# The modulation moves into the first FFN stage: sections 0 to 2 at its start, sections 3 to 8 on GpSimd and TensorE beside its products

## The chip, the core and the metric

One core of a Trainium2 chip runs the whole program. The metric is the device time in microseconds. The kernel before takes 3244.37 us, the median of three runs from 3243.7 to 3245.0 us.

## The reference, cut to what matters

One layer on 128 context tokens and 1024 latent tokens, D_MODEL 1024, D_FF 2816, all in float32. The modulation is a vector of nine sections of 1024 numbers for each of the two conditions (context and latents), and every sub-layer uses three of them.

```python
mod = (jax.nn.silu(c) @ ada_w[l] + ada_b[l]).reshape(b, 9, 1024)    # for c_ctx and for c
h = rmsnorm(x, norm_w[0]) * (1.0 + m[1]) + m[0]
x = x + 0.5 * m[2] * swiglu(h, ffn1_w13, ffn1_w2)       # first FFN: sections 0, 1, 2
h = rmsnorm(x, norm_w[1]) * (1.0 + m[4]) + m[3]
x = x + m[5] * token_mixer(h, ...)                      # sections 3, 4, 5
h = rmsnorm(x, norm_w[2]) * (1.0 + m[7]) + m[6]
x = x + 0.5 * m[8] * swiglu(h, ffn2_w13, ffn2_w2)       # sections 6, 7, 8
```

## The kernel before

`program` (L1936 to L1963) runs stage after stage with a barrier between any two (L81): the modulation, ffn1, the mixer's stages, ffn2, the final norm. The activations are held transposed in `x`: eight tiles of 128 features by 1152 tokens, in three chunks of CH = 384 tokens (CH and NC, L20 and L21).

**The modulation** (`modulation`, L94 to L224) handles one section at a time. SP loads a section of `ada_w` with four DMAs of 1 MB into one of two buffers (L121), and x (L126) between sections 1 and 2. TensorE multiplies the silu of both conditions by it, 16 matmuls in four column groups (L176), each two instructions in the trace. ScalarE copies the rows to SBUF (L154), and TensorE turns them with a 0/1 matrix `select`, eight small matmuls (L187), so that a section stands along the partitions. VectorE adds the bias (L210). After the ninth section it makes the scales and gates (L218, L221).

**ffn1 and ffn2** are one function, `hidden_stage` (L348), with the norm as its first part. `Norm` (L227): ScalarE, VectorE and GpSimd square x, TensorE sums the squares over the features with a matrix of ones (L275), ScalarE takes the root (L286), VectorE the reciprocal (L335). Then tile after tile of x, 24 in all: VectorE makes `x_normed` (L340), ScalarE the high half `h_hi` (L297), GpSimd the full value `h_full` (L313), and VectorE the low half `h_lo` by subtraction (L325). Products are made of high and low halves, three matmuls for each. In chunk 0 a tile has two token segments, one per condition.

The body goes over 22 tiles of D_FF in eleven pairs. A pair has six up blocks (par, c), of 48 matmuls each (L558), and three down blocks, of 48 matmuls (L573); the order on TensorE is up (0,0), down of the pair before chunk 2, up (0,1), up (0,2), up (1,0), up (1,1), down chunk 0, up (1,2), down chunk 1 (DOWN, L369). Pair 0 has no first down block. Around them, per up block: ScalarE's silu (L606), VectorE's product g (L609), ScalarE's `g_hi` (L440), VectorE's `g_lo` (L494), and the splits of the next weight tiles into `whi` (L428) and `wlo` (L466), which SPLITS (L366) hands out. VectorE adds a down block to x with the gate (L474). SP loads the weight tiles a, b and d, one ahead (L402). GpSimd does nothing in the body of ffn1. Each engine's program runs in order, and the semaphores alone tie them together.

Of the kernel before, what the change touches and what calls it, by code (L numbers as in the profile page):

```python
# [93 lines left out]
def modulation(kit):  # L94

    nc = kit.nc
    loaded_vec, loaded_x, loaded_select = kit.sem("vec_loaded"), kit.sem("x_loaded"), kit.sem("select_loaded")  # L100
    loaded = [[kit.sem(f"ada_loaded{p}{g}") for g in range(4)] for p in range(2)]
    cleared, silu_ready, ones_ready = kit.sem("cond_cleared"), kit.sem("silu_ready"), kit.sem("ones_ready")
    rows_done, rows_ready, turned = kit.sem("mod_rows_done"), kit.sem("mod_rows_ready"), kit.sem("mod_turned")
    section_added, section_done = kit.sem("section_added"), kit.sem("section_done")
    HALF = D // 2
    with ExitStack() as ctx:
        raw = ctx.enter_context(nc.sbuf_tensor("ada_raw", [P, 2, 4, 2, D], F32))
        cs = ctx.enter_context(nc.sbuf_tensor("cond_silu", [P, KT, 32], F32))
        rows = ctx.enter_context(nc.sbuf_tensor("mod_rows", [P, 2, 2, HALF], F32))
        select = ctx.enter_context(nc.sbuf_tensor("select", [P, 2], F32))  # L110
        block = ctx.enter_context(nc.Block())

        @block.sync
        def _(sp):
            sp.dma_start(kit.vec[:], kit.dram["vec"]).then_inc(loaded_vec, 16)

            def section(i, par, first=False):
                if not first:
                    kit.hold(sp, rows_done, i * 2 - 2)
                for g in range(4):  # L120
                    sp.dma_start(raw[:, par, g], kit.dram["ada_w"][i, g]).then_inc(loaded[par][g], 16)  # L121
            section(0, 0, True)
            sp.dma_start(select[:], kit.dram["select"]).then_inc(loaded_select, 16)
            section(1, 1, True)
            for k in range(KT):
                sp.dma_start(kit.x[:, k, :], kit.dram["xT"][k]).then_inc(loaded_x, 16)  # L126
            section(2, 0)
            with sp.Fori(1, 4) as i:
                for par in range(2):
                    section(i * 2 + (1 + par), 1 - par)  # L130
            sp.wait_ge(loaded_x, 16 * KT)

        @block.gpsimd
        def _(pool):
            pool.memset(cs[:], 0.0).then_inc(cleared, 1)
            pool.memset(kit.ones[:], 1.0).then_inc(ones_ready, 1)
            pool.memset(kit.eps[:, 0:1], NORM_EPS).then_inc(ones_ready, 1)
            pool.memset(kit.eps[:, 1:2], GN_EPS).then_inc(ones_ready, 1)

        @block.scalar  # L140
        def _(act):
            act.wait_ge(loaded_vec, 16)
            act.wait_ge(cleared, 1)
            a = PACK["c"][0]
            for cond in range(2):
                nc.scalar.activation(cs[:, :, cond], kit.vec[:, a + 8 * cond:a + 8 * cond + 8],
                                     ACT.Silu).then_inc(silu_ready, 1)

            def section(i, par, first=False):
                for half in range(2):  # L150
                    act.wait_ge(rows_done, i * 2 + (half + 1))
                    if not first and half == 0:
                        act.wait_ge(turned, i - 1)
# [10 lines left out]
        def _(pe):  # L164
            pe.wait_ge(silu_ready, 2)

            def section(i, rank, par, first=False):
# [3 lines left out]
                if not first:  # L171
                    pe.wait_ge(rows_ready, i * 2 - 2)
# [1878 lines left out]
```

## Time and profile before

| | us |
|---|---|
| median of 3 runs | 3244.37 |
| the profiled execution, its own time | 3243.18 |
| its span | 3241.4 |
| last section of the modulation added | 119.3 |
| first FFN product | 149.3 |
| last FFN product of ffn1 ends | 989.0 |

The page of the profile gives the busy share of each engine and, in 40 slices of 81 us, when it was busy and how busy the DMA engines were. TensorE is busy 92% of the span, VectorE 45%, ScalarE 24%, GpSimd 10%. PEclk is the granted TensorE clock; 1.00 is 2.4 GHz. PE is TensorE, PEld its weight loads, DVE VectorE, ACT ScalarE, POOL GpSimd, SP SyncE. The order of time gives start and duration of each instruction or run of equal ones; the DMA issue of an engine is listed under SPq, and its duration is that of the issue, not of the transfer.

### The profile page before, as it was taken

The numbers are of one execution on the slowest core, as the hardware profiler recorded it, in microseconds if no ns is written. First come the engines' busy times: TensorE is split into PE (matmuls) and PEld (weight loads), VectorE is DVE, ScalarE is ACT, GpSimd is POOL, SyncE is SP. The second block draws the span as 40 slices with busy tenths as digits, with TensorE's granted clock in tenths as the row PEclk, the third lists the DMA queues.
The fourth block names the chain that finished last, engine by engine and source line by source line (L and its number), as shares of the span: only waits on it lengthen the run. The fifth ranks groups of instructions, "written<-read, shape, count | busy, mean of one in ns | idle before, by whom it ended". The sixth has DMA issues, their size and how long they took to land. (4 is left out here: it accounts for less than half of the span.)

```text
span 3241.4 us, 56108 instructions
## 1 busy us (share of the span) xinstructions
PE 2975.2 (92%) x23416; PEld 2787.4 (86%) x23416; DVE 1456.3 (45%) x2475; ACT 776.3 (24%) x1296; POOL 332.4 (10%) x318
## 2 busy tenths in 40 slices
PE   4799999999996999998699976989979999999997
PEld 1399999999995988998588954779879999999996
DVE  0344333334436345432688855335553343443335
ACT  0321111111113233443133334212141111111112
POOL 0310000000004001122121212012240000000000
PEclk7899999999998999999799998989999999999999
DMA  9411111111102334443444321242111111111111
GB/s 399 159 40 39 39 39 39 57 50 42 39 13 90 129 107 149 164 156 138 116 109 96 68 107 33 71 172 93 44 36 46 39 39 39 39 39 39 39 40 64
DMA packets 182217, 263.72 MB, mean 81 GB/s; under 512 B 78128, under 2 KB 133424, under 8 KB 177456
## 3 DMA queue, kind: packets, MB, share of 16 engines
q1 hardware_dynamic: 182064, 261.52, 24.5%
q8 instruction: 116, 1.90, 0.2%
q14 instruction: 37, 0.30, 0.0%
HBM read 206.35 MB, written 55.12 MB: 81 GB/s over the span
## 5 line engine op out<-in xcount | busy, mean ns | idle before, releaser
L474 DVE SCALAR_TENSOR_TENSOR x<-bank,gate,x 128x128 f32<-128x128 f32 (+1 forms) x832 | 411.6, 516 | 209.6 <-PE bank L573 209.1
L609 DVE TENSOR_TENSOR g_ffn<-act_out_ffn,bank 128x384 f32<-128x384 f32 x132 | 73.2, 554 | 742.7 <-ACT act_out_ffn L606 742.7
L558 PE MATMUL bank<-h_hi_ffn,wlo_a_ffn 128*128 128x384 f32 x1056 | 356.9, 338 | 21.2 <-DVE h_lo_ffn L325 11.3
L606 ACT ACTIVATE act_out_ffn<-bank 128x384 f32<-128x384 f32 x132 | 65.0, 492 | 1246.1 <-PE bank L558 1246.0
L558 PE MATMUL bank<-h_lo_ffn,whi_a_ffn 128*128 128x384 f32 x1056 | 355.8, 337 | 0.0
L558 PE MATMUL bank<-h_hi_ffn,whi_a_ffn 128*128 128x384 f32 x1056 | 355.5, 337 | 0.0
L573 PE MATMUL bank<-g_hi_ffn,wlo_d_ffn 128*128 128x384 f32 x1056 | 352.9, 334 | 2.4 <-DVE g_lo_ffn L494 2.4
L573 PE MATMUL bank<-g_hi_ffn,whi_d_ffn 128*128 128x384 f32 x1056 | 352.7, 334 | 0.0
L558 PE MATMUL bank<-h_hi_ffn,whi_b_ffn 128*128 128x384 f32 x1056 | 352.7, 334 | 0.0
L573 PE MATMUL bank<-g_lo_ffn,whi_d_ffn 128*128 128x384 f32 x1056 | 352.7, 334 | 0.0
L558 PE MATMUL bank<-h_hi_ffn,wlo_b_ffn 128*128 128x384 f32 x1056 | 352.7, 334 | 0.0
L558 PE MATMUL bank<-h_lo_ffn,whi_b_ffn 128*128 128x384 f32 x1056 | 352.7, 334 | 0.0
L1066 PE MATMUL bank<-h_hi_mix,wlo_in 128*128 128x384 f32 x840 | 290.7, 346 | 24.0 <-DVE h_lo_mix L325 17.7
L1066 PE MATMUL bank<-h_hi_mix,whi_in 128*128 128x384 f32 x840 | 283.7, 338 | 0.0
L1066 PE MATMUL bank<-h_lo_mix,whi_in 128*128 128x384 f32 x840 | 283.5, 338 | 0.0
L558 PEld LDWEIGHTS bank<-h_hi_ffn,wlo_a_ffn 128*128 128x128 f32 x1056 | 200.7, 190 | 23.6 <-DVE h_lo_ffn L325 13.4
L558 PEld LDWEIGHTS bank<-h_lo_ffn,whi_a_ffn 128*128 128x128 f32 x1056 | 200.8, 190 | 0.0
L573 PEld LDWEIGHTS bank<-g_hi_ffn,wlo_d_ffn 128*128 128x128 f32 x1056 | 198.2, 188 | 3.0 <-DVE g_lo_ffn L494 3.0
L558 PEld LDWEIGHTS bank<-h_hi_ffn,whi_a_ffn 128*128 128x128 f32 x1056 | 200.5, 190 | 0.0
L558 PEld LDWEIGHTS bank<-h_hi_ffn,whi_b_ffn 128*128 128x128 f32 x1056 | 198.3, 188 | 0.0
L558 PEld LDWEIGHTS bank<-h_hi_ffn,wlo_b_ffn 128*128 128x128 f32 x1056 | 198.3, 188 | 0.0
L573 PEld LDWEIGHTS bank<-g_lo_ffn,whi_d_ffn 128*128 128x128 f32 x1056 | 198.2, 188 | 0.0
(236 smaller groups left out, 4915.9 us busy)
## 6 DMA issues: line engine op xcount, KB each, us to landing
ada_raw<-in_ada_w SPq DMA_DIRECT2D x36, 1024.0 KB, 11.6
raw_a_ffn<-in_ffn_w SPq DMA_DIRECT2D x44, 512.0 KB, 4.6
raw_b_ffn<-in_ffn_w SPq DMA_DIRECT2D x44, 512.0 KB, 4.5
raw_d_ffn<-in_ffn_w SPq DMA_DIRECT2D x44, 512.0 KB, 3.6
raw_in<-in_w_in SPq DMA_DIRECT2D x35, 512.0 KB, 5.1
mix<-row_out SPq DMA_DIRECT2D x23, 576.0 KB, 3.1
sc_ar<-streams SPq DMA_DIRECT2D x36, 256.0 KB, 3.5
sc_bkv<-streams SPq DMA_DIRECT2D x36, 256.0 KB, 4.2
```

The costliest lines, as they stand in the source:

```text
L474: ins = nc.vector.scalar_tensor_tensor(xs, kit.banks[4 + d % 4][:, a:b], kit.gate[:, gate, d, cond:cond + 1], xs, ALU.mult, ALU.add)
L558: mm = nc.tensor.matmul(kit.banks[2 * slot + j][:, 0:CH], w[q][:, par, cols], v[:, k, toks], start=(k == 0 and m == 0), stop=(k == ku - 1 ...
L573: mm = nc.tensor.matmul(kit.banks[4 + d % 4][:, 0:CH], w["d"][:, par, cols], v[par][:, c], start=(par == 0 and m == 0), stop=(par == 1 and ...
L606: return self.nc.scalar.activation(out, a, ACT.Silu)
L609: self.nc.vector.tensor_tensor(g32, act_out, b, ALU.mult).then_inc(g32_ready, 1)
L1066: mm = nc.tensor.matmul(bank[3 * par + c][:, 0:CH], wt[:, par, cols], v[:, k, toks], start=(k == 0 and m == 0), stop=(k == KT - 1 and m == 2))
```

## The change

The stage of the modulation is gone. A class `Opening`, which derives from `Norm`, is passed to ffn1 as its norm part.

Sections 0 to 2 open the stage. SP loads vec, x, section 0, section 1, select, the first a and b tiles, and section 2, and then waits for section 2's row products before the first d tile. TensorE makes the statistics of all three chunks, the rows of sections 0 and 1, their turns, and the rows of section 2; the norm needs only sections 0 and 1. VectorE makes all three reciprocals first (`inv_rms` has three slots now), adds the sections, makes the first scales, splits the first a and b, and then runs the norm. The turn of section 2 stands behind the first up block, and its gate behind VectorE's step (0, 2).

Sections 3 to 8 are made by GpSimd in units: a section has four units of 256 columns, and a unit eight steps, one for each 128 rows of `ada_w`. A step loads a 128x256 piece by a DMA that GpSimd issues itself, two ahead; multiplies it by the silu of both conditions (128x512 in all); and adds the product to the unit's sum (not in the first step). TensorE sums a unit over the partitions with 128x128 of the sum as weights and one column of ones, four matmuls a unit, in bank 7 beside the down blocks' columns. In pair i, 3 to 8, the first two units of section i are summed behind up block (0,2) and the other two behind (1,0), each after a wait for GpSimd; VectorE adds the section in its step (1,0), and TensorE waits for that before its down block of (1,1). The loop over pairs is three loops now on TensorE and VectorE (pairs 1 and 2, 3 to 8, the rest). The scales and gates of the mixer and ffn2 are made behind pair 8. Of the buffers, `g_hi0` and `g_lo0` stand elsewhere, and some lie over the loads of the opening.

```diff
-def modulation(kit):
...
 class Norm:
+    opens = False
...
+class Opening(Norm):
+    opens = True
+    QW = D // 4
+    SUMS = {(0, 2): (0, 1), (1, 0): (2, 3)}
+    AT = 384
+    TURN_BANK = (7, 4, 7)
...
+    def third(self, scratch):
+        self.raw_third = scratch.enter_context(self.nc.sbuf_tensor("ada_third", [P, 4, 2, D], F32))
+        self.cs = scratch.enter_context(self.nc.sbuf_tensor("cond_silu_wide", [P, KT, 32], F32))
+    def beside(self, buf):
+        self.acc, self.product = buf("section_sum", [P, 4, 2, self.QW]), buf("section_product", [P, 2, self.QW])
+        self.raw = buf("ada_beside", [P, 2, self.QW])
...
+    def load_section(self, sp, i):
+        for g in range(4):
+            sp.dma_start(self.raw_of(i)[:, g], self.kit.dram["ada_w"][i, g]).then_inc(self.ada_loaded[i], 16)
+    def load_first(self, sp):
+        kit = self.kit
+        sp.dma_start(kit.vec[:], kit.dram["vec"]).then_inc(self.S["vec_loaded"], 16)
+        for k in range(KT):
+            sp.dma_start(kit.x[:, k, :], kit.dram["xT"][k]).then_inc(self.x_loaded[k // 2], 16)
+        for i in range(2):
+            self.load_section(sp, i)
+        sp.dma_start(self.select[:], kit.dram["select"]).then_inc(self.S["select_loaded"], 16)
+    def load_third(self, sp):
+        self.load_section(sp, 2)
+        sp.wait_ge(self.S["mod_rows_done"], 6)
+    def rows_of(self, pe, i, banks):
+        pe.wait_ge(self.ada_loaded[i], 64)
+        for half in range(2):
+            for kk in range(2):
+                for g in range(4):
+                    mm = self.nc.tensor.matmul(self.kit.banks[banks[half]][32 * g:32 * g + 32, :], self.cs[:, 2 * g + kk, :],
+                                               self.raw_of(i)[:, g, kk, half * 512:(half + 1) * 512],
+                                               start=(kk == 0), stop=(kk == 1))
+            mm.then_inc(self.S["mod_rows_done"], 1)
+    def turn(self, pe, i):
+        pe.wait_ge(self.S["mod_rows_ready"], i * 2 + 2)
+        for mt in range(KT):
+            mm = self.nc.tensor.matmul(self.kit.banks[self.TURN_BANK[i]][:, 2 * mt:2 * mt + 2],
+                                       self.rows[:, i % 2, mt // 4, (mt % 4) * P:(mt % 4 + 1) * P], self.select[:],
+                                       start=True, stop=True)
+        mm.then_inc(self.S["mod_turned"], 1)
+    def tensor(self, pe):
+        pe.wait_ge(self.S["ones_ready"], 3)
+        super().tensor(pe)
+        pe.wait_ge(self.S["silu_ready"], 4)
+        self.rows_of(pe, 0, (0, 1))
+        self.rows_of(pe, 1, (2, 3))
+        pe.wait_ge(self.S["select_loaded"], 16)
+        pe.wait_ge(self.rms_ready, 3)
+        self.turn(pe, 0)
+        self.turn(pe, 1)
+        self.rows_of(pe, 2, (5, 6))
+    def third_turn(self, pe):
+        pe.wait_ge(self.S["section_added"], 1)
+        self.turn(pe, 2)
+    def sum_up(self, pe, i, quarters, x_added):
+        pe.wait_ge(x_added, i * 24)
+        for q in quarters:
+            pe.wait_ge(self.S["unit_ready"], i * 4 + (q - 11))
+            for mt in range(2):
+                for cond in range(2):
+                    at = self.AT + 2 * (2 * q + mt) + cond
+                    mm = self.nc.tensor.matmul(self.kit.banks[7][:, at:at + 1], self.acc[:, q, cond, mt * P:(mt + 1) * P],
+                                               self.kit.ones[:, 0:1], start=True, stop=True)
+            mm.then_inc(self.S["unit_turned"], 1)
...
+        self.squares(0, act, 0)
+        self.squares(0, act, 2)
+        act.wait_ge(S["ones_ready"], 3)
+        for c in range(NC):
+            root(c)
+        self.copy_rows(act, 0, (0, 1))
+        self.copy_rows(act, 1, (2, 3))
+        split_weights()
+        act.wait_ge(S["scale_ready"], 1)
+        for m in range(NC * KT):
+            c, k = divmod(m, KT)
+            act.wait_ge(self.xn_ready, m + 1)
+            for cond, a, b in segments(c):
+                ins = nc.scalar.activation(self.at(self.h_hi, k, c)[:, a:b], self.xn[:, m % 2, a:b], ACT.Identity,
+                                           bias=kit.mod[:, 0, k, cond:cond + 1], scale=kit.scale[:, 0, k, cond:cond + 1])
+            ins.then_inc(self.hi_ready, 1)
+            if m == KT + 1:
+                self.copy_rows(act, 2, (5, 6))
...
+    def sections(self, pool):
+        nc, S, QW = self.nc, self.S, self.QW
+        pool.wait_ge(self.h_ready, NC * KT)
+        pool.wait_ge(S["mod_turned"], 3)
+        pool.wait_ge(S["silu_ready"], 4)
+        units = [(i, q) for i in range(3, 9) for q in range(4)]
+        def load(n):
+            u, k = divmod(n, KT)
+            i, q = units[u]
+            pool.dma_start(self.raw[:, n % 2], self.kit.dram["ada_w"][i, k // 2, :, k % 2, q * QW:(q + 1) * QW])\
+                .then_inc(self.unit_loaded[n % 2], 16)
+        load(0)
+        load(1)
+        step = 0
+        for u in range(len(units)):
+            if u >= 4:
+                pool.wait_ge(S["unit_turned"], u - 3)
+            acc = self.acc[:, u % 4]
+            for k in range(KT):
+                n = KT * u + k
+                pool.wait_ge(self.unit_loaded[n % 2], 16 * (n // 2 + 1))
+                if step:
+                    pool.wait_ge(S["unit_step"], step)
+                nc.gpsimd.tensor_tensor(self.product[:] if k else acc,
+                                        self.raw[:, n % 2:n % 2 + 1].broadcast_to([P, 2, QW]),
+                                        self.silu[:, k].rearrange("p (c t) -> p c t", t=1).broadcast_to([P, 2, QW]),
+                                        ALU.mult).then_inc(S["unit_step"], 1)
+                step += 1
+                pool.wait_ge(S["unit_step"], step)
+                if n + 2 < KT * len(units):
+                    load(n + 2)
+                if k:
+                    ins = nc.gpsimd.tensor_tensor(acc, acc, self.product[:], ALU.add).then_inc(S["unit_step"], 1)
+                    step += 1
+            pool.wait_ge(S["unit_step"], step)
+            pool.sem_inc(S["unit_ready"], 1)
+    def add_section(self, dve, i):
+        nc, kit, S = self.nc, self.kit, self.S
+        a = PACK["ada_b"][0]
+        bias = kit.vec[:, a:a + 9 * KT].rearrange("p (i m c) -> p i m c", i=9, c=1)
+        if isinstance(i, int):
+            dve.wait_ge(S["mod_turned"], i + 1)
+            out, bias, bank, at = kit.mod[:, i:i + 1], bias[:, i:i + 1], self.TURN_BANK[i], 0
+        else:
+            dve.wait_ge(S["unit_turned"], i * 4 - 8)
+            out, bias, bank, at = kit.mod[:, bass.ds(i, 1)], bias[:, bass.ds(i, 1)], 7, self.AT
+        nc.vector.tensor_tensor(out, kit.banks[bank][:, at:at + 16].rearrange("p (i m c) -> p i m c", i=1, c=2),
+                                bias.broadcast_to([P, 1, KT, 2]), ALU.add).then_inc(S["section_added"], 1)
...
+    def third_gate(self, dve):
+        self.add_section(dve, 2)
+        dve.wait_ge(self.S["section_added"], 3)
+        self.gates(0, self.S["gate_ready"])
+        dve.wait_ge(self.S["gate_ready"], 1)
...
+        self.squares(1, dve, 0)
+        for c in range(NC):
+            dve.wait_ge(self.rms_ready, c + 1)
+            nc.vector.reciprocal(self.inv[:, c], self.inv[:, c]).then_inc(self.inv_ready, 1)
+        dve.wait_ge(S["vec_loaded"], 16)
+        self.add_section(dve, 0)
+        self.add_section(dve, 1)
+        dve.wait_ge(S["section_added"], 2)
+        self.scales(0, S["scale_ready"])
+        split_weights()
+        dve.wait_ge(self.inv_ready, NC)
...
+            if opening:
+                opening.load_first(sp)
+            for q in "ab":
                 load(q, 0, True)
+            if opening:
+                opening.load_third(sp)
+            load("d", 0, True)
...
+                if opening and early and (par, c) == (0, 2):
+                    opening.third_gate(dve)
...
+                        if beside and (par, c) == (1, 0):
+                            opening.add_section(dve, i)
             pair(0, early=True)
+            if opening:
+                with dve.Fori(1, 3) as i:
+                    pair(i)
+                with dve.Fori(3, 9) as i:
+                    pair(i, beside=True)
+                opening.finish(dve)
+                with dve.Fori(9, pairs - 1) as i:
+                    pair(i)
...
+            if opening:
+                opening.sections(pool)
...
-            def pair(i, early=False):
+            def pair(i, early=False, beside=False):
                 for par in range(2):
                     for c in range(NC):
                         up(i, par, c, early)
+                        if opening and early and (par, c) == (0, 0):
+                            opening.third_turn(pe)
+                        if beside and (par, c) in opening.SUMS:
+                            opening.sum_up(pe, i, opening.SUMS[par, c], x_added)
+                        if opening and (early or beside) and (par, c) == (1, 1):
+                            pe.wait_ge(opening.S["section_added"], 3 if early else i + 1)
                         if (par, c) in DOWN:
                             back, chunk = DOWN[par, c]
                             if not (early and back):
                                 down(i - back, chunk, early)
             pair(0, early=True)
-            with pe.Fori(1, pairs) as i:
-                pair(i)
+            if opening:
+                with pe.Fori(1, 3) as i:
+                    pair(i)
+                with pe.Fori(3, 9) as i:
+                    pair(i, beside=True)
+                with pe.Fori(9, pairs) as i:
+                    pair(i)
+            else:
+                with pe.Fori(1, pairs) as i:
+                    pair(i)
             down(pairs - 1, NC - 1)
 
...
         with kit.stage():
-            modulation(kit)
-        with kit.stage():
-            ffn(kit, "ffn1", 0, "ffn1_w13", "ffn1_w2")
+            ffn(kit, "ffn1", 0, "ffn1_w13", "ffn1_w2", first=True)
```

## Rows read from the trace of the kernel before

**Rows 1.** The page, busy time, and 40 slices of the span.

```profile
span 3241.4 us, 56108 instructions
...
PE 2975.2 (92%) x23416; PEld 2787.4 (86%) x23416; DVE 1456.3 (45%) x2475; ACT 776.3 (24%) x1296; POOL 332.4 (10%) x318
...
DMA  9411111111102334443444321242111111111111
```

**Rows 2.** Order of time, 0 to 62 us: start, duration, engine, line, operation.

```profile
5.92 14.77 SPq L126 DMA_DIRECT2D x<-in_xT  x8
13.93 5.63 PE L176 MATMUL bank<-ada_raw,cond_silu 128*32 128x512 f32 x32 [13.93 <-DMA ada_raw<-in_ada_w]
...
24.51 5.34 PE L176 MATMUL bank<-ada_raw,cond_silu 128*32 128x512 f32 x32 [4.95 <-DMA ada_raw<-in_ada_w]
...
29.78 1.95 PE L187 MATMUL bank<-select,mod_rows 128*128 128x2 f32 x16
...
46.00 4.96 PE L176 MATMUL bank<-ada_raw,cond_silu 128*32 128x512 f32 x32 [14.28 <-DMA ada_raw<-in_ada_w]
```

**Rows 3.** Order of time, 95 to 165 us.

```profile
119.25 0.17 DVE L210 TENSOR_TENSOR mod<-bank,vec 128x16 f32<-128x16 f32 x1 [2.61 <-PE bank L187]
...
121.27 0.34 SPq L402 DMA_DIRECT2D raw_a_ffn<-in_ffn_w  x1
...
121.66 0.43 SPq L402 DMA_DIRECT2D raw_b_ffn<-in_ffn_w  x1
...
127.87 1.22 DVE L466 TENSOR_TENSOR wlo_a_ffn<-raw_a_ffn,whi_a_ffn 128x1024 fp32r<-128x1024 f32 x1
...
129.00 1.22 DVE L466 TENSOR_TENSOR wlo_b_ffn<-raw_b_ffn,whi_b_ffn 128x1024 fp32r<-128x1024 f32 x1
...
133.17 1.70 DVE L340 TENSOR_TENSOR x_normed_n<-x,inv_rms_n 128x384 f32<-128x384 f32 x2
...
136.33 12.24 POOL L313 TENSOR_SCALAR h_full_n<-x_normed_n,scale,mod 128x128 f32<-128x128 f32 x16
...
149.29 0.44 PE L558 MATMUL bank<-h_hi_ffn,wlo_a_ffn 128*128 128x384 f32 x1
```

**Rows 4.** Busy time, granted clock and DMA share by stretch.

```profile
core 0: us, PE busy (x) PEld busy (x) DVE busy (x) ACT busy (x) POOL busy (x), PEclk, DMA share, GB/s
...
29.70:31.80 2.10, 2.03 (x20) 1.86 (x16) 0.00 (x0) 0.60 (x1) 0.00 (x0) 1.00 1.02 413
...
163.50:173.90 10.40, 10.38 (x47) 10.38 (x48) 8.61 (x13) 4.14 (x6) 6.27 (x6) 0.77 0.00 0
...
275.00:350.00 75.00, 75.00 (x435) 75.00 (x434) 29.27 (x51) 11.92 (x19) 0.00 (x0) 1.00 0.13 42
350.00:425.00 75.00, 75.00 (x434) 75.00 (x434) 29.27 (x51) 11.93 (x19) 0.00 (x0) 1.00 0.14 42
```

**Rows 5.** Order of time on PE, the end of ffn1.

```profile
988.64 0.34 PE L573 MATMUL bank<-g_hi_ffn,whi_d_ffn 128*128 128x384 f32 x1
```

**Rows 6.** Waits of PE, 149 to 240 us: us in total, times, longest.

```profile
PE bank L558 <- DVE h_lo_ffn L325: 5.6, 1, 5.6
PE bank L558 <- DVE g_ffn L609: 4.6, 1, 4.6
```

**Rows 7.** Order of time, 155 to 200 us.

```profile
163.38 2.55 DVE L335 RECIPROCAL inv_rms_n<-rms_n 128x384 f32<-128x384 f32 x1
...
163.52 0.69 PE L558 MATMUL bank<-h_hi_ffn,wlo_a_ffn 128*128 128x384 f32 x1 [5.64 <-DVE h_lo_ffn L325]
...
177.15 0.56 DVE L325 TENSOR_TENSOR h_lo_ffn<-h_full_n,h_hi_ffn 128x384 fp32r<-128x384 f32 x1 [0.47 <-POOL h_full_n L313]
```

**Rows 8.** Order of time in the scan stage, 1780 to 1806 us.

```profile
1781.98 0.51 SPq L1142 DMA_DIRECT2D sc_bkv<-v_back  x1
...
1804.11 0.67 DVE L1309 TENSOR_TENSOR sc_kr<-bank,sc_masks 128x512 f32<-128x512 f32 x1
...
1805.03 1.27 POOL L1216 TENSOR_TENSOR sc_n<-sc_nk,sc_masks 128x512 f32<-128x512 f32 x1
```

**Rows 9.** Order of time in the merge stage, 2119 to 2127 us.

```profile
2119.04 1.01 POOL L1863 TENSOR_TENSOR gated_parts<-act_out_merge,gates 128x384 f32<-128x384 f32 x1 [133.14 <-ACT act_out_merge L1848]
2120.13 1.01 POOL L1867 TENSOR_TENSOR g_merge<-gated_parts 128x384 f32<-128x384 f32 x1
```

**Rows 10.** The merge's line L1863: duration min/median/max in ns.

```profile
L1863 POOL TENSOR_TENSOR gated_parts<-act_out_merge,gates x24: 1005/1014/1560, 2119.0 to 2320.1; 128x384 f32<-128x384 f32 x24
```

**Rows 11.** DVE by line, 240 to 940 us: busy us, mean ns, idle before.

```profile
L494 DVE TENSOR_TENSOR g_lo_ffn<-g_ffn,g_hi_ffn 128x384 fp32r<-128x384 f32 x57 | 31.5, 553 | 17.9 <-ACT g_hi_ffn L440 17.9
L466 DVE TENSOR_TENSOR wlo_b_ffn<-raw_b_ffn,whi_b_ffn 128x1024 fp32r<-128x1024 f32 x19 | 23.2, 1222 | 3.9 <-ACT whi_b_ffn L428 3.9
L466 DVE TENSOR_TENSOR wlo_a_ffn<-raw_a_ffn,whi_a_ffn 128x1024 fp32r<-128x1024 f32 x19 | 23.2, 1219 | 0.0
L466 DVE TENSOR_TENSOR wlo_d_ffn<-raw_d_ffn,whi_d_ffn 128x1024 fp32r<-128x1024 f32 x18 | 22.1, 1226 | 7.1 <-ACT whi_d_ffn L428 7.1
```

More of the change, by code:

```diff
@@ L387, in hidden_stage @@
         raw = {q: buf(f"raw_{q}", [P, width[q]]) for q in "ab"}
+        whi, wlo = ({q: buf(f"{n}_{q}", [P, 2, width[q]], F32R) for q in "ab"} for n in ("whi", "wlo"))
+        if opening:
+            with ExitStack() as scratch:
+                opening.third(scratch)
+        g_hi, g_lo = [buf("g_hi0", [P, NC, CH], F32R), g_hi1], [buf("g_lo0", [P, NC, CH], F32R), g_lo1]
         raw_d = buf("raw_d", [P, ahead, D])
         raw_of = lambda q, slot: raw_d[:, slot % ahead] if q == "d" else raw[q][:]
-        whi = {q: buf(f"whi_{q}", [P, 2, width[q]], F32R) for q in kinds}
-        wlo = {q: buf(f"wlo_{q}", [P, 2, width[q]], F32R) for q in kinds}
+        whi["d"], wlo["d"] = buf("whi_d", [P, 2, D], F32R), buf("wlo_d", [P, 2, D], F32R)
         act_out, g32 = buf("act_out", [P, 2, CH]), buf("g32", [P, 2, CH])
@@ L506, in _, with pair @@
                 first_weights()
-            def pair(i, early=False, last=False):
+            def pair(i, early=False, last=False, beside=False):
                 for par in range(2):
@@ L511, in pair @@
                         step(i, par, c, early, last)
+                        if beside and (par, c) == (1, 0):
+                            opening.add_section(dve, i)
             pair(0, early=True)
-            with dve.Fori(1, pairs - 1) as i:
-                pair(i)
+            if opening:
[6 more added lines that the diff above has]
+                    pair(i)
+            else:
+                with dve.Fori(1, pairs - 1) as i:
+                    pair(i)
             pair(pairs - 1, last=True)
@@ L585, in _ @@
             pair(0, early=True)
-            with pe.Fori(1, pairs) as i:
-                pair(i)
+            if opening:
+                with pe.Fori(1, 3) as i:
[4 more added lines that the diff above has]
+                    pair(i)
+            else:
+                with pe.Fori(1, pairs) as i:
+                    pair(i)
             down(pairs - 1, NC - 1)
@@ L609, in vector, with ffn @@
         self.nc.vector.tensor_tensor(g32, act_out, b, ALU.mult).then_inc(g32_ready, 1)
-def ffn(kit, tag, n, w13, w2):
+def ffn(kit, tag, n, w13, w2, first=False):
     def norm(ctx, scratch):
+        if first:
+            return Opening(kit, ctx, scratch, tag)
         h_hi = ctx.enter_context(kit.nc.sbuf_tensor(f"h_hi_{tag}", [P, KT, T], F32R))
```

240 lines of the change are left out of this document (120 added, 120 removed).

## The prediction

> **What bounds the kernel now.** I read the busy shares first: TensorE (PE) is at 92% of the span, and the only slice in which the DMA engines are nearly full is the beginning [rows 1]. The order of time of that beginning shows why. The row products of section 0 start at 13.93 us, those of section 1 at 24.51 and those of section 2 at 46.00, each released by its DMA, so 10.6 us for a 4 MB section, and 21.5 us for x and a section, which leaves 10.9 us for x [rows 2]. The modulation is therefore limited by its loads, and nothing of the FFN overlaps it. Its last section is added at 119.25 us, the norm's first x_normed comes at 133.17 us and the first FFN product at 149.29 us [rows 3]. From there TensorE is full: two stretches of 75 us hold 435 and 434 products, 0.1726 us each, with TensorE's granted clock at 1.00, its 2.4 GHz level [rows 4]. A block of 48 products is 8.29 us, a pair of F-tiles has nine blocks (six up, three down), so 74.6 us, and eleven pairs are 820.8 us. The last product of ffn1 ends at 988.98 us [rows 5], 839.7 us after its first, so 18.9 us are stalls and slow starts: waits of 5.6 and 4.6 us show in the list of waits [rows 6]. VectorE, ScalarE and GpSimd are idle much of the time there, GpSimd wholly [rows 4].
>
> So two quantities decide: when the first FFN product starts, and whether anything added afterwards makes TensorE late.
>
> **The start: a gain.** Loads in the new order are x (10.9 us), then sections 0 and 1. From the anchor at 13.93 us (vec and one section) section 1 has landed at 13.93 + 10.9 + 10.6 = 35.4 us. Its row products and hand-over take 5.3 us (24.51 to 29.78) [rows 2], to 40.7. Two turns at 1.95 us each follow [rows 2], to 44.6; the two adds, their waits and the two scale instructions about 0.6, to 45.2. The split of the first a and b tiles on VectorE comes next in its program, 2.35 us (127.87 to 130.22) [rows 3], to 47.6. The squares and all three roots and reciprocals fit under the section loads: x is there by about 15 us, and before they took from 121.3 to about 133. The chunk-0 norm then runs at GpSimd's pace: from its first h_full at 136.33 to the first product 12.95 us [rows 3], and 0.65 us from x_normed to h_full. First product: 47.6 + 0.65 + 12.95 = 61.2 us instead of 149.3, **a gain of 88.1 us**. The third section lands about 13 us after section 1 (a, b and 4 MB), its row products are done by about 54 us, before the first FFN product, so they cost nothing unless the loads are over 7 us late. SP waits for these products before the first d tile, which is needed only at the first down block, some 40 us later: nothing.
>
> **The start stalls.** The turn of section 2 stands on TensorE behind the first up block (+2.0). The second block waited for chunk 1 until 163.52, 14.2 us after the first [rows 7]; the same eight tiles plus ScalarE's two row copies make it about 13.3 (-0.9). Chunk 2 loses its reciprocal, 2.55 us [rows 7] (-2.5). TensorE is idle before the first block now; a block begun after such an idle ran from 163.52 with a granted clock of 0.77 and took 10.4 us [rows 4] (+2.1 against 8.29). That leaves -1.3 in all, and 17.6 us of stalls in place of 18.9.
>
> **What is put on TensorE later.** Each of sections 3 to 8 adds 16 matmuls with one column. The nearest row is a turn: 8 matmuls are 16 instructions in 1.95 us, 0.122 each, at granted clock 1.00 [rows 2, 4]. Six sections: 192 x 0.122 = 23.4 us, all on the path, since TensorE is full. For the 12 switches in and out I add 0.3 each: **27 us**. Bounds: 20 and 34 (with the 0.84 us idle in front of a turn instead of 0.3). The new waits: DVE's add of a section is queued ahead of its later steps, but its input comes 2 us after the up block it follows, while VectorE is still splitting tiles; the wait for the add at the block (1,1) has a whole up block of cover. Both nothing. The two additional loops I take as nothing (the present one turns without TensorE going idle [rows 4]); bounds 0 to 3.
>
> **Does GpSimd keep up?** This is the term that decides. The work is 24 units of 8 steps; a step is a 128x512 multiply, a DMA issue and (not in a unit's first step) a 128x512 add, in strict order with waits on its own semaphore: 192 multiplies, 192 issues, 168 adds. GpSimd's 128x512 TENSOR_TENSOR with a broadcast operand takes 1.27 us [rows 8]. The merge shows a dependent pair on GpSimd with its self-wait: 2119.04 + 1.01 to 2120.13, a gap of 0.08 us [rows 9]. So 192 x 1.35 + 168 x 1.35 = 259.2 + 226.8 = 486 us for the arithmetic. The issue of a DMA by GpSimd is in no row. SP's issues took 0.34 to 0.43 us for the FFN's weights [rows 3] and 0.51 us for a tile of the scan [rows 8]; 0.34 is my low end, and the high end is the 14.77/8 = 1.85 us of SP's issues of x with a full queue [rows 2]. Between them: GpSimd needs 1.27 us for a 128x512 operation of which VectorE does the like in 0.67 [rows 8], a factor of 1.9; times 0.47, the middle of 0.43 and 0.51, it is **0.9 us**, which is what I take, as an estimate. 192 x 0.9 = 172.8 us. For VectorE in the same memory I add 0.15 us a step, 28.8 us: in ffn1 its operations with two SBUF inputs (g_lo and the three wlo) sum to 31.5 + 23.2 + 23.2 + 22.1 = 100 us of 700 [rows 11], 0.5 us per step, and only part of them falls where GpSimd is ready to start. Together **688 us**, 28.7 a unit. Ends: 552 us (0.34 and no contention) and 870 us (1.85).
>
> How much it may take: GpSimd starts when the norm is through (177.71 [rows 7] is 28.4 us after the first product; less the reciprocal and the 0.9: 25 us) plus 2 us for the first landing: 27.1 us after the first product. TensorE asks for the last unit after 76 blocks: 8 in pair 0, 63 in pairs 1 to 7, 5 in pair 8. 76 x 8.29 = 630.0, plus 17.6, plus the sums before it, 24.8: 672.4 us. The window is 645.3 us. At 688 us **TensorE waits 42 us**: some 7 in pair 7 (20 units, ready at 600 us, wanted at 593), the rest in pair 8. At pair 3 only four units are wanted, after some 277 us: no wait.
>
> The Trainium skill, page "DMA: Bandwidth & Descriptors", section "Latency and other measured facts", gives about 1 us to the first byte of a DMA from the GpSimd queue, because its cores write the descriptors in software; no row here shows it. Were 1.0 us the time that each issue keeps GpSimd, the time would be 19 us above the forecast.
>
> **Sum.** 3243.2 (profiled execution; span 3241.4) - 88.1 - 1.3 + 27 + 42.3 = 3223.1; the median of the runs is 1.2 above that execution: **3224 us**. Past ffn1 nothing changes. With no wait at all the same sum is 3182, and each 0.1 us of an issue is worth 19 us from 0.68 us up, so this forecast is as good as the 0.9.
>
> **Rivals.**
> (A) GpSimd keeps up: an issue under 0.68 us, or one that overlaps the arithmetic. Wait 0, 3182 us. For it: SP's 0.34 to 0.51 us [rows 3, 8]; against: the arithmetic alone is 486 of the 645 us. Chance 0.22.
> (B) The forecast, GpSimd late by less than the change gains: an issue of 0.68 to 0.97 us, 3183 to 3237 us. Chance 0.32.
> (C) GpSimd late by more than the change gains, from an issue of 1.04 us up: at 1.2 us TensorE waits 100 us and the time is 3244.4 - 62.4 + 100 = 3282 us. Chance 0.22. Between B and C, within 0.2% of the time before: 0.09.
> (D) The issue is as in B, but the memory is shared the hard way: each two-input operation of VectorE holds GpSimd for its whole length, 0.55 us a step instead of 0.15, so 192 x 0.4 = 77 us more: 3301 us. The longest multiply in the merge took 1.56 us against a median of 1.01 [rows 10], a whole VectorE operation of 0.55 more; most took the median. Chance 0.15.
> The Trainium skill, page "SBUF — State Buffer", section "Who interferes with whom", has the rule that would bring D about: the two engines share one port pair as an exclusive lock, and a VectorE instruction with two SBUF inputs and a GpSimd one that reads block each other fully. By that rule it is up to 3301; the median near 1.01 bears it out only now and then.
>
> **How the numbers follow.** Faster by over 0.2% (about what a measurement of this kernel can tell from no change): A and B, 0.54. Same: 0.09. Slower: C and D, 0.37. The range reaches from A with the sums at their low bound (3182 less 7) to D: 3175 to 3301; B alone is 3183 to 3237.
>
> **What would show it.** The first product of an up block at about 61 us (over 70: the start is wrong). 192 one-column product instructions in the FFN with about 23 us. On GpSimd 192 multiplies and 168 adds at 1.27 to 1.4 us, and from multiply to add, across the issue, about 0.9 us of idle: under 0.7 makes A right, over 1.04 C. TensorE waiting for GpSimd's section_sum in pairs 7 and 8 only, about 42 us. The prediction is wrong as a whole if waits appear elsewhere in ffn1, as on wlo tiles that GpSimd delays.

## The result and the profile after

The changed kernel takes 3315.52 us (median of four runs, 3312.3 to 3318.8) against 3244.68 us for the kernel before on the same chip: a ratio of 1.0218, 95% interval 1.0201 to 1.0236. It is 71 us slower. The forecast was 3224 us with a range of 3175 to 3301, so both the sign and the range are wrong.

In 40 slices of the span, each digit the busy share in tenths, TensorE before was nearly full from the third slice on:

```profile
PE   4799999999996999998699976989979999999997
```

The page of the changed kernel (slices of 83 us): TensorE's line has holes in slices 6 to 11, the granted clock falls with them, and GpSimd works in two stretches with a hole between (slices 3 and 4). A second DMA queue appears (q0), the one that GpSimd fills.

```profile
span 3317.0 us, 56526 instructions
...
PE   7999987679798799999599996979979999999998
...
POOL 4821888888201201222112113012240000000000
PEclk8999988889899899999699998989999999999999
...
q0 software_dynamic: 9216, 25.18, 2.7%
```

The opening, in order of time: the row products of section 1, the adds, the first x_normed and the first FFN product (line 759 is line 558 of before). It stands at 59.92 us, where [rows 3] has 149.29.

```profile
35.59 3.64 PE L292 MATMUL bank<-ada_first,cond_silu_wide 128*32 128x512 f32 x32 [0.92 <-DMA ada_first<-in_ada_w]
...
43.41 0.17 DVE L458 TENSOR_TENSOR mod<-bank,vec 128x16 f32<-128x16 f32 x1 [2.02 <-PE bank L300]
...
46.05 1.02 DVE L515 TENSOR_TENSOR x_normed_n<-x,inv_rms_n 128x384 f32<-128x384 f32 x2
...
59.92 0.69 PE L759 MATMUL bank<-h_hi_ffn,wlo_a_ffn 128*128 128x384 f32 x1 [5.82 <-DVE h_lo_ffn L495]
```

The waits of TensorE from 60 to 1060 us (us in total, times, longest), which answer to [rows 6], and below them the row that holds the answer, GpSimd's from 100 to 900 us. The wait of 5.8 us for `h_lo` stands in front of the first product; in [rows 6] it stood behind the first block. POOLq L444 is the `sem_inc` that declares a unit ready; L329 is TensorE's sum of a unit.

```profile
PE bank L329 <- POOLq L444: 114.9, 5, 25.8
PE bank L759 <- DVE h_lo_ffn L495: 5.8, 1, 5.8
PE bank L759 <- DVE g_ffn L824: 2.9, 1, 2.9
...
POOL section_sum_ffn L432 <- PE bank L329: 127.6, 1, 127.6
```

TensorE waits five times for GpSimd, once in each of pairs 4 to 8, 114.9 us in all, and before that GpSimd waits once for TensorE, 127.6 us. GpSimd's order of time shows when: its fifth unit starts at 321.02, as soon as TensorE has summed the first at 320.00 in pair 3.

```profile
321.02 1.04 POOL L432 TENSOR_TENSOR section_sum_ffn<-ada_beside_ffn,cond_silu 128x512 f32<-128x512 f32 x1 [127.57 <-PE bank L329]
322.36 0.58 POOL L418 DMA_DIRECT2D ada_beside_ffn<-in_ada_w  x1 [0.30 <-POOL section_sum_ffn L432]
322.96 1.05 POOL L432 TENSOR_TENSOR section_product_ffn<-ada_beside_ffn,cond_silu 128x512 f32<-128x512 f32 x1
```

The line of the change that does it is the wait at the head of each unit, `if u >= 4: pool.wait_ge(S["unit_turned"], u - 3)`: the sum has four slots, and unit 4 needs the slot of unit 0, which TensorE gives back only in pair 3. Of the 645 us that I had counted as GpSimd's window, 128 are idle, and in each of pairs 3 to 8 four units are wanted. A unit takes 26.6 us (in the order of time the first multiply of a unit starts at 400.45 and that of the next at 427.07), four take 106 us, and a pair with its sums about 79.

Where the 75.6 us of span went, by three stretches of each trace (one trace a kernel; the experiments follow below). "Behind ffn1" is the span less the end of the last product of ffn1. The last two columns are the two waits above.

| kernel | first product at | ffn1 from first to last product | behind ffn1 | GpSimd idle for a slot | TensorE waits for units |
|---|---|---|---|---|---|
| before | 149.3 | 839.7 | 2252.4 | | |
| the changed kernel | 59.9 | 994.2 | 2262.9 | 127.6 | 114.9 |
| opening_only | 59.6 | 843.1 | 2260.2 | | |
| sums_only | 59.5 | 864.2 | 2262.0 | | |
| late1 | 59.1 | 995.7 | 2259.9 | 204.0 | 114.1 |
| spread | 60.2 | 873.2 | 2260.0 | none | 1.3 |
| before_again | 146.8 | 839.8 | 2259.3 | | |
| no_issue | 59.6 | 876.7 | 2260.4 | 151.5 | 5.7 |
| spread_sums | 59.4 | 867.7 | 2258.7 | | |
| ring2 | 60.1 | 1133.8 | 2260.0 | 281.9 | 245.4 |

The start gains 89.4 us, ffn1 loses 154.5, and 10.5 are lost behind ffn1.

### The profile page after: what moved, and what is told of

The parts are those of the page before. It is cut to its first block and busy times, and to the rows that moved or that the text cites. A ratio compares the mean times of both kernels' runs of the same rounds, so it can differ in the third digit from the quotient of the medians.

```text
span 3317.0 us, 56526 instructions
## 1 busy us (share of the span) xinstructions
PE 2978.8 (90%) x23320; PEld 2816.9 (85%) x23320; DVE 1503.2 (45%) x2475; ACT 770.0 (23%) x1286; POOL 877.9 (26%) x870
## 5 line engine op out<-in xcount | busy, mean ns | idle before, releaser
L759 PE MATMUL bank<-h_hi_ffn,wlo_a_ffn 128*128 128x384 f32 x1056 | 365.2, 346 | 19.7 <-DVE g_ffn L824 8.2
L759 PE MATMUL bank<-h_lo_ffn,whi_a_ffn 128*128 128x384 f32 x1056 | 362.5, 343 | 0.0
L759 PE MATMUL bank<-h_hi_ffn,whi_a_ffn 128*128 128x384 f32 x1056 | 362.4, 343 | 0.0
L759 PEld LDWEIGHTS bank<-h_hi_ffn,wlo_a_ffn 128*128 128x128 f32 x1056 | 204.9, 194 | 22.1 <-issue 8.8
L441 POOL TENSOR_TENSOR section_sum_ffn<-section_sum_ffn,section_product_ffn 128x512 f32<-128x512 f32 x168 | 221.0, 1315 | 3.7
```

The lines of the kernel that those rows point to most:

```text
L441: ins = nc.gpsimd.tensor_tensor(acc, acc, self.product[:], ALU.add).then_inc(S["unit_step"], 1)
L759: mm = nc.tensor.matmul(kit.banks[2 * slot + j][:, 0:CH], w[q][:, par, cols], v[:, k, toks], start=(k == 0 and m == 0), stop=(k == ku - 1 ...
```

## The experiments

Theory R: the four slots let GpSimd work only four units ahead; then it idles until pair 3 and is too slow for four units a pair. Theory W, the prediction's: GpSimd's whole work stands against the whole window. All ratios are to runs of the kernel before taken beside them on the same chip.

**opening_only: what the opening alone gives.**

```diff
+        for n in (1, 2):
+            self.nc.vector.tensor_scalar(self.kit.mod[:, 3 * n:3 * n + 3], self.kit.mod[:, 0:3], 1.0, None, ALU.mult)\
+                .then_inc(self.S["section_added"], 1)
...
-            if opening:
-                opening.sections(pool)
...
-                        if beside and (par, c) in opening.SUMS:
-                            opening.sum_up(pe, i, opening.SUMS[par, c], x_added)
```

> The changed kernel without sections 3 to 8: GpSimd makes no units, TensorE sums none, and the modulation of the mixer and of the second FFN is copied from sections 0 to 2, so these two stages compute with other numbers at the same cost. It prices the new opening alone. The first product comes 89.4 us earlier than before (59.9 for 149.3), and the start stalls show 8.7 us of waits for 10.2: all theories expect about 3244.7 - 89.4 - 1.5 = 3154 us. If it is 3165 or more, the opening itself gives something back later (two more loops, a colder clock), which no wait in the trace of the changed kernel shows.

Measured: 3167.14 us, ratio 0.9745 (0.9729 to 0.9761), 84 us faster than the 3251.57 us of the kernel before beside it. The 3154 us that were expected are missed by 13 us, and the sign named for that, 3165 or more, came true. Some 7 us of it are in the comparison: the kernel before takes 3251.57 us beside these runs and took 3244.68 beside those of the changed kernel. Of the rest 4.9 us are in ffn1, which is 3.4 us longer than before's where 1.5 us less were expected, though the waits for VectorE at its start fell from 10.2 to 2.8 us. Two things hide in the 3.4. From first product to the start of pair 1 TensorE needs 74.6 us instead of 80.9. Every later pair takes 75.86 us instead of 74.88, because its six up blocks take 8.48 us each instead of 8.32. The kernel before starts 435 products in 75 us at full clock [rows 4]; opening_only starts 429 (the same columns):

```profile
215.00:290.00 75.00, 75.00 (x429) 75.00 (x429) 29.17 (x50) 11.80 (x18) 0.00 (x0) 1.00 0.13 42
```

GpSimd is idle in this stretch and the clock is at 1.00, so neither is the reason. The up blocks of ffn2 still take 8.32 us. All the changed kernels traced have the 8.48 in ffn1; what makes it, no run tells.

**sums_only: the price of TensorE's sums.** GpSimd's loop over the units is replaced by one constant.

```diff
+        nc.gpsimd.memset(self.acc[:], 0.001).then_inc(S["unit_ready"], 1)
...
-            pe.wait_ge(self.S["unit_ready"], i * 4 + (q - 11))
+            pe.wait_ge(self.S["unit_ready"], 1)
```

> As the changed kernel, but GpSimd fills the four slots of the sum with a constant once, and TensorE sums them at the usual places without waiting for units; the sections 3 to 8 are therefore constants plus bias. It prices the 192 one-column products and their switches. My prediction's term: 27 us above the kernel with the opening only, so 3181 us; bounds 20 to 34. What then separates the changed kernel (3315.5) from this one, about 134 us, is GpSimd: 115 us of waits that the trace shows, and some 19 us that would be TensorE running at its lower clock after each of five waits. Rival, contention: part of the 134 is VectorE delayed by GpSimd's reads (wlo at 1.7 us for 1.22); then sums_only is well above 3181 only if it is not GpSimd.

Measured: 3188.42 us, ratio 0.9806 (0.9790 to 0.9822), 21.3 us above opening_only on the same chip where 27 were expected; the 7 us above the 3181 are the same difference between the comparisons. ffn1 is 21.1 us longer than in opening_only (864.2 to 843.1). In order of time the sums stand between the products without a gap, 16 instructions in 1.84 us, 0.115 each:

```profile
321.11 1.84 PE L329 MATMUL bank<-ones,section_sum_ffn 128*128 128x1 f32 x16
331.21 1.84 PE L329 MATMUL bank<-ones,section_sum_ffn 128*128 128x1 f32 x16
```

In the medians 127 us separate this kernel from the changed one (134 if each is set against the kernel before beside it); in ffn1 of the two traces it is 130.0 us. Since this kernel lacks only GpSimd's units, those come from what GpSimd does or makes TensorE wait for.

**late1: one pair later, the test of R against W.** VectorE's loops and its add of a section move by one pair as well.

```diff
-            pe.wait_ge(self.S["unit_ready"], i * 4 + (q - 11))
+            pe.wait_ge(self.S["unit_ready"], i * 4 + (q - 15))
...
-                with pe.Fori(1, 3) as i:
+                with pe.Fori(1, 4) as i:
                     pair(i)
-                with pe.Fori(3, 9) as i:
+                with pe.Fori(4, 10) as i:
                     pair(i, beside=True)
```

> The changed kernel with each section summed one pair later (section i in pair i + 1, pairs 4 to 9). Theory R, the ring: the sum has four slots, so GpSimd makes four units, then stands idle until the first sum, and from there needs 4 x 26.6 = 106 us for the four units of each pair of 75 + 4 us. The first sum comes one pair later, GpSimd idles some 75 us longer (203 us for 128), and TensorE waits as before in the five pairs that follow, 115 us in all: the time stays at 3315 us within 5. Theory W, the window, as my prediction had it: GpSimd works through from the norm on, and 75 us more of window take at least 75 us of the waiting away: 3240 us or less.

Measured: 3316.11 us, ratio 1.0203 (1.0186 to 1.0220). Waits of GpSimd and TensorE in late1:

```profile
POOL section_sum_ffn L432 <- PE bank L329: 204.0, 1, 204.0
...
PE bank L329 <- POOLq L444: 114.1, 5, 26.4
```

75 us more of window change nothing: GpSimd idles 76 us longer, and TensorE waits five times again, as long as before. W is refuted, R gave both numbers.

**spread: the same work and slots, taken evenly.** Three units in each of pairs 1 to 8, behind block (1,0); VectorE adds three sections at a time.

```diff
-        for q in quarters:
-            pe.wait_ge(self.S["unit_ready"], i * 4 + (q - 11))
+        if p == 0:
+            pe.wait_ge(self.S["section_added"], j + 3)
+        for u in range(3 * p, 3 * p + 3):
+            pe.wait_ge(self.S["unit_ready"], j * 12 + (u + 1))
...
-                with pe.Fori(1, 3) as i:
-                    pair(i)
-                with pe.Fori(3, 9) as i:
-                    pair(i, beside=True)
+                with pe.Fori(0, 2) as j:
+                    for p in range(4):
+                        pair(j * 4 + (p + 1), beside=(j, p))
```

> The same units by GpSimd, the same four slots, but TensorE takes three units in each of the pairs 1 to 8 behind up block (1,0), and VectorE adds three sections at once in pairs 4 and 8. Nothing of GpSimd's work is left out. Theory R: the slots come free all along, GpSimd never idles, 24 x 26.6 = 638 us from 27 us after the first product, against the last sum wanted about 660 us after it: waits under 15 us, and 3181 + 10 = about 3190 us. Theory W or a plain lack of speed of GpSimd: the units are no faster and wanted no later than in the changed kernel, so the waits stay near 115 us and the time near 3310. Theory C, contention: the waits go, but the time stays above 3205 because GpSimd slows VectorE's splits.

Measured: 3193.64 us, ratio 0.9827 (0.9807 to 0.9847), a ratio with its interval wholly below 1: faster than before, with nothing left out of the work. TensorE's waits, the first of them in front of the first product:

```profile
PE bank L763 <- DVE h_lo_ffn L500: 6.1, 1, 6.1
PE bank L763 <- DVE g_ffn L829: 3.2, 1, 3.2
PE bank L330 <- POOLq L443: 1.3, 1, 1.3
PE bank L778 <- DVE g_lo_ffn L687: 1.2, 1, 1.2
```

GpSimd never waits for a slot. Not one instruction of its 192 steps was taken out, so at the speed that GpSimd has, the order in which its results are taken makes the difference between 115 us of waits and 1.3. Spread changes two things of that order at once, the first sum (pair 1, not 3) and the number of sums a pair (three, not four); no run changes one of them alone.

**before_again: the time behind ffn1.**

> The kernel before, unchanged, on the chip of this call, for its trace. In the traces of all changed kernels the time behind the first FFN is 7.5 to 10.5 us longer than in the trace of before (2252.4 us), and most of it lies in the scan stage, whose code is the same. If it is the chip, this trace shows some 2260 us behind ffn1 too; if the change causes it, 2252.

Measured: 3247.7 us (one run), and 2259.3 us behind ffn1. The unchanged kernel thus differs by 6.9 us there between two traces, and the two changed kernels traced on this same chip, no_issue and spread_sums, have 2260.4 and 2258.7: here the change costs nothing behind ffn1. The other experiments have 2259.9 to 2262.0. For the changed kernel itself, 2262.9, that leaves 3.6 us above this trace and 10.5 above the first; its traced execution was 3.3 us above its median. What makes the remainder stays open.

**no_issue: GpSimd's rate.**

```diff
-                pool.wait_ge(self.unit_loaded[n % 2], 16 * (n // 2 + 1))
+                pool.wait_ge(self.unit_loaded[n % 2], 16)
...
-                if n + 2 < KT * len(units):
-                    load(n + 2)
```

> The changed kernel, its order of sums untouched (pairs 3 to 8, four slots), but GpSimd issues only the first two of its 192 loads and multiplies these two pieces over and over, so sections 3 to 8 are other numbers. It prices GpSimd's issue and tests the rate: a unit took 26.6 us, of which 8 x 0.88 (0.58 busy, 0.30 in front) are the issue, so 19.6 us a unit and 78 us for the four of a pair, against some 79 us for a pair with its sums. Theory R: the waits vanish nearly (under 10 us) although GpSimd still stands idle until pair 3 (some 150 us), and the time is 3188 to 3200 us. If the waits were for the landing of the pieces or for VectorE's lock and not for the plain sum of GpSimd's instructions, they would stay above 50 us, and the time above 3240.

Measured: 3196.49 us, ratio 0.9839 (0.9822 to 0.9855); TensorE waits 5.7 us, in pairs 6 to 8, and GpSimd idles 151.5 us for the first slot. So the rate is part of the cause as well: with a faster GpSimd the changed kernel's own schedule works, nearly. A unit takes 20.8 us, 83 us for four against 79 for a pair, where 19.6 and 78 were expected. Without its issues GpSimd's arithmetic got longer, a multiply from 1.12 to 1.14 us and an add from 1.32 to 1.40, and taking the issues out saves 5.8 us a unit and not the 7.0 of their rows.

**spread_sums: what of spread is GpSimd's.** Spread with the constant of sums_only in place of the units.

> As spread, but GpSimd only fills the slots with a constant, and TensorE doesn't wait for units. Spread's TensorE takes 9.0 us longer over ffn1 than that of sums_only (873.2 to 864.2 us), of which 1.3 are a wait and 0.5 an issue. If the rest is GpSimd beside it (VectorE's wlo at 1.7 us for 1.22, DMA), this run has about 865 us in ffn1 and 3188 us in all, as sums_only. If it is the program itself, a loop body of four pairs instead of one, it stays near 871 us and 3194.

Measured: 3188.70 us, ratio 0.9816 (0.9800 to 0.9833); ffn1 867.7 us. Of the 9.0 us that spread's ffn1 is above that of sums_only, 3.5 are there without GpSimd's units and 5.5 come on top with them, 1.3 of these a wait. The split is not firmer than 1.5 us: pair 0, the same in all of them, takes 74.6 or 76.1 us up to the start of pair 1, as a stretch of 3.4 us at half clock falls into it or not, and it does in sums_only and in spread. An undisturbed pair of spread and of spread_sums takes the same 78.38 us, so GpSimd's work as such does not slow TensorE. Both expectations were half right.

**ring2: two slots instead of four.**

```diff
-            if u >= 4:
-                pool.wait_ge(S["unit_turned"], u - 3)
-            acc = self.acc[:, u % 4]
+            if u >= 2:
+                pool.wait_ge(S["unit_turned"], u - 1)
+            acc = self.acc[:, u % 2]
...
-                                               self.acc[:, q, cond, mt * P:(mt + 1) * P],
+                                               self.acc[:, q % 2, cond, mt * P:(mt + 1) * P],
```

> The changed kernel with two slots of GpSimd's sum in place of four, everything else the same; it computes the same. Theory R: the slots are what lets GpSimd work ahead. With two, the two units wanted behind block (1,0) can only be begun when TensorE has summed the first two behind (0,2), one block of 8.3 us earlier: 2 x 26.6 - 8.3 = 45 us of waiting in each of six pairs, 264 to 270 us in all, and none behind (0,2), since 66 us lie before it. The time is 3315 + 150 = about 3465 us, with the colder clock up to 3480. If the slots don't matter (GpSimd's sum of work against the window), it stays at 3315 us.

Measured: 3457.18 us (two runs), ratio 1.0643 (1.0612 to 1.0674). TensorE waits twelve times, twice a pair and both times behind block (1,0), once for each of the two units that are made late, 41 us a pair where 45 were expected:

```profile
PE bank L329 <- POOLq L444: 245.4, 12, 23.6
...
POOL section_sum_ffn L432 <- PE bank L329: 281.9, 6, 181.4
```

Only the number of slots was changed, and 142 us followed (139.6 in ffn1 of the traces). That shows the slots as part of the cause from the other side. No run has more than four slots, so that more of them would cure the changed kernel is argued, not shown.

## Why the prediction was wrong

**The start: right.** 59.9 us for the first product against 61.2; the gain is 89.4 us for 88.1 (the kernel before has 149.3 us in one trace and 146.8 in the other). Sections landed and were multiplied as counted, and the third section's row products cost nothing.

**The start stalls: too small, and a slip in the sum.** My four terms, +2.0, -0.9, -2.5 and +2.1, add up to +0.7 and not to the -1.3 that I carried on; the first was left out. Measured, pair 0 is 6.4 us shorter in opening_only. What I had at nothing is the 0.98 us that each of the ten later pairs is longer (the up blocks of 8.48 us), 9.8 us in all. The two together are the 3.4 us by which ffn1 grows.

**The sums: 21.1 us against 27.** The 0.122 us an instruction was nearly right (0.115, 22.1 us for 192); the 0.3 us for each switch is not to be seen in the total.

**GpSimd's time: right, a little high.** GpSimd's groups in ffn1, from 80 to 1000 us (busy us, mean ns | idle before):

```profile
L441 POOL TENSOR_TENSOR section_sum_ffn<-section_sum_ffn,section_product_ffn 128x512 f32<-128x512 f32 x168 | 221.0, 1315 | 3.7
L432 POOL TENSOR_TENSOR section_product_ffn<-ada_beside_ffn,cond_silu 128x512 f32<-128x512 f32 x168 | 188.2, 1120 | 27.9 <-DMA ada_beside_ffn<-in_ada_w 7.2
L418 POOL DMA_DIRECT2D ada_beside_ffn<-in_ada_w x192 | 111.0, 578 | 60.1 <-POOL section_product_ffn L432 49.0 <-POOL section_sum_ffn L432 7.1 <-issue 3.0
```

An issue is 0.58 us and 0.30 in front of it, the wait for the multiply that frees its buffer: 0.88 where I took 0.9. (The Trainium skill, page "DMA: Bandwidth & Descriptors", section "Latency and other measured facts", has about 1 us to the first byte, which is a different quantity; no run here shows it.) Multiplies are 1.12 us and adds 1.32, for 1.27. A unit took 26.6 us against 28.7.

**The window: this step failed.** "GpSimd starts when the norm is through (...): 27.1 us after the first product. TensorE asks for the last unit after 76 blocks (...) The window is 645.3 us." Both ends are right: GpSimd's first multiply starts 26.4 us after the first product, and in sums_only, where nothing waits for GpSimd, the last unit is summed 668 us after it. What was left out is that GpSimd may not use the time between. With the measured 26.6 us a unit, 24 units are 638 us, and the comparison with 645 us would give no wait at all, 3182 us: better numbers would have made this forecast worse. I had asked of the waits that the change adds on TensorE and on VectorE who stands behind them, and not of the one that it adds on GpSimd, though it stands in the diff. Had I followed it with my own numbers: 30 blocks of 8.29 us and 17.6 us of stalls put the first sum 266 us after the first product (it was at 260), 20 units of 28.7 us follow, so the last is ready at 840; it is wanted at 672, and TensorE waits some 168 us, for 3182 + 168 = 3350 us, slower than before. With the measured 260 and 26.6 us it is 792, and the last sum was made at 854.88 us (795.0 after the first product). TensorE waited 114.9 us where I had 42, in pairs 4 to 8 and not in 7 and 8 alone. The rivals all put the price of GpSimd's instructions in question, and none its schedule. The issue, 0.88 us, lies where rival B has it, so the slower result is not C's or D's doing, and it lies outside the range because no rival had this mechanism. The profiled execution is 95.7 us above the 3223.1 of my sum: 72.6 are these waits, 15.1 what they cost besides, 4.7 the stalls, 10.5 the time behind ffn1, less 5.9 of the sums and 1.3 of the start.

**The waits cost more than themselves.** ffn1 of the changed kernel is 994.2 us: 843.1 of opening_only, 21.1 of the sums, 114.9 of waits, and 15.1 more. The granted clock shows where that lies. Stretches of the changed kernel around a wait (us, busy of PE, PEld, DVE, ACT, POOL, clock, DMA share, GB/s), then the same stretch of spread:

```profile
410.20:426.90 16.70, 0.00 (x0) 0.00 (x0) 6.24 (x4) 2.42 (x3) 14.44 (x15) 0.62 0.40 125
...
426.90:435.00 8.10, 8.09 (x28) 8.10 (x29) 0.17 (x1) 0.00 (x0) 6.83 (x8) 0.51 0.13 34
```

```profile
426.90:435.00 8.10, 8.10 (x49) 8.10 (x48) 5.93 (x16) 1.53 (x3) 7.01 (x7) 1.00 0.17 49
```

After 16.7 us of waiting TensorE runs at its lower level, 1.2 GHz, and starts 28 products in 8.1 us, eight of them the short ones of a sum. At 2.4 GHz they would have taken 8 x 0.115 + 20 x 0.173 = 4.4 us, so 3.7 us are lost here. The same can be read pair by pair, from the first product of one to that of the next: less their waits, pairs 4 to 8 take 82.9, 82.8, 81.5, 82.5 and 82.4 us, against 79.12 for each of them in sums_only, 16.6 us in all. Behind the five waits the clock stays at its lower level for 7.9, 7.7, 4.9, 7.0 and 6.5 us, and half of that is 17.0. Pair 0 gives 1.5 us back, by its stretch at half clock that sums_only has and this trace has not; that makes the 15.1. GpSimd's presence is not in it. In pair 3 it works and nobody waits, and TensorE starts as many products as in sums_only without it (the changed kernel, then sums_only):

```profile
290.00:365.00 75.00, 75.00 (x442) 75.00 (x441) 31.92 (x49) 11.80 (x18) 36.95 (x39) 1.00 0.22 65
```

```profile
290.00:365.00 75.00, 75.00 (x442) 75.00 (x442) 27.35 (x48) 11.80 (x18) 0.00 (x0) 1.00 0.13 43
```

**VectorE pays more for the shared memory than GpSimd.** I added 0.15 us a step on GpSimd's side. Its multiply has a median of 1.04 us and a mean of 1.11, its add 1.26 us at the shortest and 1.32 in the mean, so some 0.08 to 0.13 us a step by these rows (an estimate): the term was about right, and rival D's 0.55 did not come. VectorE's lines from 140 to 740 us, in spread and in sums_only:

```profile
L687 DVE TENSOR_TENSOR g_lo_ffn<-g_ffn,g_hi_ffn 128x384 fp32r<-128x384 f32 x46 | 47.5, 1033 | 14.8 <-ACT g_hi_ffn L631 14.8
L657 DVE TENSOR_TENSOR wlo_b_ffn<-raw_b_ffn,whi_b_ffn 128x1024 fp32r<-128x1024 f32 x15 | 30.1, 2009 | 0.9 <-ACT whi_b_ffn L619 0.8
...
L829 DVE TENSOR_TENSOR g_ffn<-act_out_ffn,bank 128x384 f32<-128x384 f32 x46 | 25.5, 554 | 248.9 <-ACT act_out_ffn L826 248.9
```

```profile
L649 DVE TENSOR_TENSOR g_lo_ffn<-g_ffn,g_hi_ffn 128x384 fp32r<-128x384 f32 x46 | 25.5, 555 | 14.8 <-ACT g_hi_ffn L593 14.8
...
L619 DVE TENSOR_TENSOR wlo_b_ffn<-raw_b_ffn,whi_b_ffn 128x1024 fp32r<-128x1024 f32 x15 | 18.3, 1223 | 3.1 <-ACT whi_b_ffn L581 3.1
```

The operations with two inputs in SBUF grow from 0.555 to 1.03 us and, wlo of b, from 1.22 to 2.01 (wlo of a and d to 1.56 and 1.76), while g, one of whose inputs is in a bank, keeps its 0.554. The Trainium skill, page "SBUF — State Buffer", section "Who interferes with whom", says that a VectorE instruction with two inputs in SBUF contends with GpSimd's reads, and one with at most one such input, outside its 2-port modes, does not; these rows agree. Who loses is not what rival D made of it: GpSimd is busy some 85% of the time here, and the longer operations are VectorE's. VectorE had the slack: TensorE waits for it in spread at the start and for 1.2 us at the end, as it did in the kernel before.

## What to carry to other kernels

When work goes to an idle engine as a producer, three numbers decide: its rate, the rate at which the consumer asks while it asks, and how many results the buffers hold. A head start is worth no more than the buffers hold: here 128 us of it were spent idle, and four slots, emptied late and then four at a time, cost 115 us of the bound engine, while three a pair from pair 1 on cost 1.3 us with the same slots, and a helper that needed 20.8 us a unit instead of 26.6 cost 5.7 us with the late order. Read every wait that a diff adds, that of the helper too, and ask when it is first met; and count a long wait on TensorE dearer than its length: behind each of five waits of 16.7 to 25.8 us the clock stayed at half for 4.9 to 7.9 us of work, 2.4 to 3.8 us lost each time.

## What the runs showed of the hardware

A DMA of 128 KB (128 rows of 1 KB) issued by GpSimd occupies that engine 0.58 us (0.54 to 0.72 over 192), against 0.33 to 0.43 us for the issue of a 512 KB weight tile by SP, and lands 2.6 us after its issue in the median. A GpSimd multiply of 128x512 with both inputs broadcast takes 1.04 us in the median, one with only the second broadcast 1.27 [rows 8], and an add of two plain inputs 1.30; that the repeated first input is what makes the multiply faster was not tested. A one-column product with 128x128 of weights takes 0.115 us an instruction at a granted clock of 1.00. The same kernel took 2252.4 us behind ffn1 in one trace and 2259.3 in another; differences of that size outside the stage under study had to be set aside with the kernel before, profiled again.
